# A layer's first projection from the raw stream, scaled per token where its result is read

## The reference

```python
# one layer; x is (256, 1024), norm_g[l] has 1024 weights
h = rmsnorm(x, norm_g)          # x * g / sqrt(mean(x*x) + 1e-6), the mean over a token's features
p = h @ w_in                    # (1024, 11168); its parts are, by column:
# conv branch | lora: 256 of q, 128 of kv, 32 of rope key | dilated q, k, v | gates
q_a  = rmsnorm(p_q,  q_a_norm_g)    # over 256
kv_a = rmsnorm(p_kv, kv_a_norm_g)   # over 128
... three branches (convolution, latent attention, dilated attention), their sum gated
x = x + merged @ w_o
```

## Time and profile before

| | |
|---|---|
| median of 3 runs | 1988.99 us (1988.62 to 1989.37) |
| the profiled execution | 1993.92 us, its span 1992.0 us |
| PE busy | 1888.7 us, 95% |
| DVE / ACT / POOL busy | 749.3 / 581.2 / 522.7 us |
| layers (PE's last sum of x) | to 817.0 us |

### The profile page before, as it was taken

One profiled execution on the slowest core, in us unless ns is written; L12 is line 12 of the kernel. 1 busy time (PEld: TensorE's weight loads), 2 busy tenths in 40 slices (PEclk: granted clock), 3 DMA queues, 4 the chain that ended last, 5 costly groups with the idle time before them and its releaser, 6 DMA issues.

```text
span 1992.0 us, 26961 instructions
## 1 busy us (share of the span) xinstructions
PE 1888.7 (95%) x10968; PEld 1193.8 (60%) x10968; DVE 749.3 (38%) x1417; ACT 581.2 (29%) x1051; POOL 522.7 (26%) x220
## 2 busy tenths in 40 slices
PE   7999999989999999989899999999999999999997
PEld 6779889977799899744474444343334443333443
DVE  4785563447854644544534212121112121211212
ACT  4554445445544455322412111011011110110111
POOL 5766556767674557200000000000000000000000
PEclk9999999999999999999989999999999999999999
DMA  8555333555553234621548999999999999999995
GB/s 304 191 174 207 128 107 118 205 182 201 181 194 134 97 127 170 221 85 43 206 157 367 429 427 430 428 428 429 428 429 427 428 428 428 429 428 429 428 429 234
DMA packets 111413, 563.43 MB, mean 283 GB/s; under 512 B 4768, under 2 KB 24352, under 8 KB 86464
## 3 DMA queue, kind: packets, MB, share of 16 engines
q1 hardware_dynamic: 111328, 562.21, 70.5%
HBM read 561.15 MB, written 1.05 MB: 282 GB/s over the span
## 4 chain that ended last, share of the span: by engine, by line
PE 61%; DMA 28%; DVE 7%; ACT 2%; issue 1%; SPq 0%; DVEq 0%; ACTq 0%
DMA ring<-in_e_in_dram 28%; PE bank L1708 15%; PE score L927 11%; PE bank L1698 10%; PE bank L749 4%; PE mixed L965 4%; PE bank L1675 3%; PE bank L850 2%; PE mixed L1792 1%; PE flip L1775 1%; DVE ring L2280 1%; PE bank L988 1%; PE score L1761 1%; PE score L948 1%; PE flip L1733 1%
## 5 line engine op out<-in xcount | busy, mean ns | idle before, releaser
L2087 POOL TENSOR_TENSOR w_lo<-ring,w_hi 128x1024 fp32r<-128x1024 f32 (+1 forms) x216 | 522.5, 2431 | 285.2 <-ACT w_hi L1986 284.6
L927 PE MATMUL score<-ring,space 128*64 128x512 f32 x2016 | 452.7, 594 | 38.4 <-DMA ring<-in_e_in_dram 37.2
L927 PEld LDWEIGHTS score<-ring,space 128*64 128x64 f32 x2016 | 141.6, 137 | 338.4 <-issue 248.6
L1986 ACT ACTIVATE w_hi<-ring 128x1024 fp32r<-128x1024 f32 (+1 forms) x216 | 226.8, 1051 | 219.3 <-PE bank L1708 120.5
L1708 PE MATMUL bank<-h_hi,w_hi 128*128 128x256 f32 x896 | 261.9, 292 | 0.0
L1708 PE MATMUL bank<-h_lo,w_hi 128*128 128x256 f32 x896 | 254.2, 284 | 0.0
L1708 PE MATMUL bank<-h_hi,w_lo 128*128 128x256 f32 x896 | 254.0, 283 | 0.0
L965 PE MATMUL mixed<-ring,space 128*64 128x512 f32 x1024 | 226.8, 595 | 0.3 <-ACT space L1183 0.3
L1179 ACT ACTIVATE space<-space 128x512 f32<-128x512 f32 x32 | 20.2, 632 | 695.7 <-DVE space L1482 695.7
L1482 DVE TENSOR_SCALAR space<-score 128x512 f32<-128x512 f32 x32 | 22.2, 693 | 411.1 <-PE score L927 411.1
L1708 PEld LDWEIGHTS bank<-h_hi,w_hi 128*128 128x128 f32 x896 | 172.6, 193 | 4.5 <-issue 4.4
(11 more groups left out here) (341 smaller groups left out, 2351.0 us busy)
## 6 DMA issues: line engine op xcount, KB each, us to landing
ring<-in_e_in_dram SPq DMA_DIRECT2D x126, 2048.0 KB, 25.1
ring<-in_e_out_dram SPq DMA_DIRECT2D x64, 2048.0 KB, 22.1
ring<-in_w_in_dram SPq DMA_DIRECT2D x42, 2048.0 KB, 7.8
ring<-in_w_ada_dram SPq DMA_DIRECT2D x16, 1024.0 KB, 5.3
ring<-in_w_o_dram SPq DMA_DIRECT2D x6, 2048.0 KB, 8.0
ring<-in_w_qkv_dram SPq DMA_DIRECT2D x4, 2048.0 KB, 10.0
ring<-in_w_ada_dram SPq DMA_DIRECT2D x4, 2048.0 KB, 7.9
ring<-in_w_out_a_dram SPq DMA_DIRECT2D x2, 2048.0 KB, 7.9
```

The lines of the kernel that those rows point to most:

```text
L927: ins = pe.matmul(score[HALF * blk:HALF * blk + HALF, which * W:(which + 1) * W], xs[:, 2 * j + r, HALF * hh:HALF * hh + HALF], wk[:, blk ...
L1986: act.activation(split_part(w_hi, k), raw_part(k), ACT.Copy).then_inc(hi_done, 1)
L2087: pool.tensor_tensor(split_part(w_lo, k), raw_part(k), split_part(w_hi, k), ALU.subtract).then_inc(lo_done, 1)
```

## The change

Lora reads a second pair of buffers, `raw_hi` and `raw_lo`: x times the norm's weights, without the token's scale, split. ACT makes the high half of a piece (two operations), DVE the low half (two). In layer 0 pieces 0 to 2 are made before the root; in layer 1 pieces 0 and 1 stand behind the second squares of x, together with the splits of quarters 0 and 1. The normed stream is made as before, for the units behind lora; in ACT's queue the splits of quarters 3, 4, 5, 6 now stand before its pieces 0, 1, 2, 3. The token's scale as a column, `token_rs`, comes from a product of `rsx` with the identity and a sum, behind the stream's last subtraction; the squares and the reads of lora's result take it in.

```diff
+        raw_hi, raw_lo = latent_r[:, 0:DC, :], latent_r[:, DC:2 * DC, :]
+        token_rs = stat[:, 1, 0:TT]
...
-                if kind in ("lora", "out"):
-                    pe.wait_ge(hready, l * 8 + (0 if kind == "lora" else 4) + q + 1)
+                if kind == "lora":
+                    pe.wait_ge(raw_ready, l * 4 + q + 1)
+                elif kind == "out" or QUARTER[u] == 4:
+                    pe.wait_ge(hready, l * 8 + (4 if kind == "out" else 0) + q + 1)
+                x_hi, x_lo = (raw_hi, raw_lo) if kind == "lora" else (h_hi, h_lo)
...
-                            for x_, w_ in ((h_hi, w_hi), (h_hi, w_lo), (h_lo, w_hi)):
+                            for x_, w_ in ((x_hi, w_hi), (x_hi, w_lo), (x_lo, w_hi)):
                                 ins = pe.matmul(b[:, 0:n], x_[:, c, t], w_[:, k % PARTS, i, 0:n],
-                                                start=c == 0 and x_ is h_hi and w_ is w_hi,
-                                                stop=c == DC - 1 and x_ is h_lo)
+                                                start=c == 0 and x_ is x_hi and w_ is w_hi,
+                                                stop=c == DC - 1 and x_ is x_lo)
...
+            def squares_of_both(l, u, width, scales=(1.0, 1.0)):
                 act.wait_ge(squares_used, l * NG + MEAN_OF[u] + 1)
                 act.wait_ge(unit_done, done(l, u))
-                act.activation(square2[:, 0, 0:width], bank_of(u)[:, 0:width], ACT.Square)
+                act.activation(square2[:, 0, 0:width], bank_of(u)[:, 0:width], ACT.Square, scale=scales[0])
                 act.wait_ge(unit_done, done(l, u + 1))
-                act.activation(square2[:, 1, 0:width], bank_of(u + 1)[:, 0:width], ACT.Square).then_inc(squares, 1)
+                act.activation(square2[:, 1, 0:width], bank_of(u + 1)[:, 0:width], ACT.Square,
+                               scale=scales[1]).then_inc(squares, 1)
...
-                        squares_of_both(l, u, 384 if kind == "lora" else W)
+                        if kind == "lora":
+                            act.wait_ge(token_ready, l + 1)
+                            squares_of_both(l, u, 384, [token_rs[:, t:t + 1] for t in range(TT)])
+                        else:
+                            squares_of_both(l, u, W)
...
+            def raw_high(l, i):
+
+                layer_now[0] = l
+                for c in (2 * i, 2 * i + 1):
+                    ins = act.activation(raw_hi[:, c, :], x[:, c, :], ACT.Copy, scale=l_("norm_g", c, 1))
+                ins.then_inc(raw_rounded, 1)
+
             for i in range(4):
                 squares_of_x(0, i)
             act.wait_ge(ones_ready, 1)
             act.activation(stat[:, 0, 15:16], ones[:, 0:1], ACT.Sqrt)
             act.wait_ge(par_ready, 1)
+            for i in range(3):
+                raw_high(0, i)
+            split_to(0, 1)
             for l in range(LAYERS):
                 layer_now[0] = l
-                split[0] = 0
                 act.wait_ge(score_free, l * NS + 2)
                 act.activation(rsx, varx, ACT.Sqrt).then_inc(rsx_ready, 1)
+                raw_high(l, 3)
+                split_to(l, PARTS)
                 for n in range(4):
-                    split_to(l, min(n + 1, PARTS))
+                    split_to(l, PARTS + n + 1)
                     stream_high(l, n, normed_x)
                 evacuate(l, 0)
                 for u in range(HEAD, PREP):
@@ -2073,6 +2099,14 @@
                         act.wait_ge(bpar_loaded, 32)
                         act.activation(ctx_squares, ctx_x, ACT.Square).then_inc(bsquared, 1)
                     squares_of_x(l + 1, i)
+                    if l + 1 < LAYERS and i == 1:
+                        raw_high(l + 1, 0)
+                        raw_high(l + 1, 1)
+                        split[0] = 0
+                        split_to(l + 1, 2)
+                if l + 1 < LAYERS:
+                    split_to(l + 1, PARTS)
+                    raw_high(l + 1, 2)
...
+            def raw_low(l, i):
+                now, layer_now[0] = layer_now[0], l
+                dve.wait_ge(raw_rounded, l * 4 + i + 1)
+                for c in (2 * i, 2 * i + 1):
+                    ins = dve.scalar_tensor_tensor(out=raw_lo[:, c, :], in0=x[:, c, :], scalar=l_("norm_g", c, 1),
+                                                   in1=raw_hi[:, c, :], op0=ALU.mult, op1=ALU.subtract)
+                ins.then_inc(raw_ready, 1)
+                layer_now[0] = now
+
+            def token_scales(l):
+
+                own = qn[0][:, 0:T].rearrange("p (t n) -> p t n", t=TT)
+                link(dve.tensor_tensor(own, rsx.rearrange("p (t n) -> p t n", t=TT),
+                                       c_("ident").unsqueeze(1).broadcast_to([P, TT, P]), ALU.mult))
+                dve.tensor_reduce(token_rs, own, AX.X, ALU.add).then_inc(token_ready, 1)
...
-                    link(dve.tensor_copy(kpe[:, t, :], b[:, 384:416]))
-                    link(dve.tensor_scalar(q[:, 0:256], b[:, 0:256], rs[:, r:r + 1], None, ALU.mult))
-                    dve.tensor_scalar(q[:, 256:384], b[:, 256:384], rs[:, r + 1:r + 2], None,
+                    own = token_rs[:, t:t + 1]
+                    link(dve.tensor_scalar(kpe[:, t, :], b[:, 384:416], own, None, ALU.mult))
+                    link(dve.tensor_scalar(q[:, 0:256], b[:, 0:256], rs[:, r:r + 1], own, ALU.mult, ALU.mult))
+                    dve.tensor_scalar(q[:, 256:384], b[:, 256:384], rs[:, r + 1:r + 2], own, ALU.mult,
                                       ALU.mult).then_inc(free_of(u), 1)
...
+            for i in range(2):
+                raw_low(0, i)
             for l in range(LAYERS):
                 base[0] = l * PER["layer"] + start
                 steps[0] = 0
                 layer_now[0] = l
                 dve.wait_ge(scored, l * NS + 1)
                 dve.tensor_scalar(varx, score[:, 0:T], 1.0 / D, EPS, ALU.mult, ALU.add).then_inc(score_free, 1)
+                raw_low(l, 2)
                 dve.wait_ge(rsx_ready, l + 1)
                 link(dve.reciprocal(rsx, rsx))
+                raw_low(l, 3)
                 for n in range(4):
                     for c in (2 * n, 2 * n + 1):
                         ins = dve.scalar_tensor_tensor(out=normed_x[:, c, :], in0=x[:, c, :], scalar=l_("norm_g", c, 1),
@@ -2359,6 +2414,7 @@
                 stream_low(l, 3, normed_x)
                 if l == 0:
                     dve.wait_ge(loaded, 16)
+                token_scales(l)
                 for u in range(PREP):
                     evacuate(l, u)
                 for j in range(NJ + 1):
@@ -2386,6 +2442,9 @@
                 dve.wait_ge(free_of(FILL - 1), freed(l, FILL - 1))
                 dve.wait_ge(free_of(FILL - 2), freed(l, FILL - 2))
                 for u in range(FILL, NU):
+                    if l + 1 < LAYERS and u == NU - 2:
+                        raw_low(l + 1, 0)
+                        raw_low(l + 1, 1)
```

More of the change, by code:

```diff
@@ L215 @@
 CP, NCP = places(CONSTS)
-CHAINED = dict(layer=111, pair=2, job=2)
+CHAINED = dict(layer=112, pair=2, job=2)
 def slope(g, h):
@@ L452, in build @@
         hready = sem("hready")
+        raw_rounded = sem("raw_rounded")
+        raw_ready = sem("raw_ready")
+        token_ready = sem("token_ready")
         unit_done = sem("unit_done")
@@ L1866, in squares_of @@
                 act.activation(square[:, 0:width], src, ACT.Square).then_inc(squares, 1)
-            def squares_of_both(l, u, width):
+            def squares_of_both(l, u, width, scales=(1.0, 1.0)):
                 act.wait_ge(squares_used, l * NG + MEAN_OF[u] + 1)
                 act.wait_ge(unit_done, done(l, u))
-                act.activation(square2[:, 0, 0:width], bank_of(u)[:, 0:width], ACT.Square)
+                act.activation(square2[:, 0, 0:width], bank_of(u)[:, 0:width], ACT.Square, scale=scales[0])
                 act.wait_ge(unit_done, done(l, u + 1))
-                act.activation(square2[:, 1, 0:width], bank_of(u + 1)[:, 0:width], ACT.Square).then_inc(squares, 1)
+                act.activation(square2[:, 1, 0:width], bank_of(u + 1)[:, 0:width], ACT.Square,
+                               scale=scales[1]).then_inc(squares, 1)
             def root(l, u):
```

## The result

Slower by 0.57%: the ratio of the changed kernel's runs to those of before is 1.0057 with an interval of 1.0045 to 1.0068, from 8 runs each (medians 2002.17 and 1989.39 us). The profiled executions took 2001.8 and 1993.92 us, 7.9 apart (spans 2000.0 and 1992.0). A second series, on another chip, gave 1.0044 (1.003 to 1.0057). By the two ratios the loss is 9 to 11 us, by their intervals 6 to 14; the forecast was 7.5. The eight runs of the kernel before lie in two groups, five at 1988.6 to 1989.4 us and three at 1994.7 to 1995.3, and its profiled execution lies near the upper one, so the profiled pair shows less of a loss than the medians (12.8).

What follows compares the result with a forecast made beforehand. TensorE, busy for 95% of the span, was taken to bound the kernel. Waits of 2.6 (layer 1) and 3.1 (layer 0) plus clock 2.0 gave 7.7 us on 1988.99, so 1996.7, forecast as 1996.5; range 1986 to 2001.

Steps and rivals of the forecast that it cites:

- main step: In both layers, VectorE operations with two SBUF inputs wait for GpSimd's running split; one gets through between two splits.
- the lead of unit 1: Lora's earlier start without waiting for the normed stream: 16.95 instead of 18.5 in layer 0, 3.0 us ahead in layer 1.
- Q7: Quarter 7, the eighth of the layer, on TensorE; forecast 2.6 us late in layer 1, 2.4 to 3.8 in layer 0.
- Waits, 5.7 us in the sum: Delay at Q7 from VectorE's waits behind splits: 2.6 us in layer 1 and 3.1 in layer 0.
- the second of the two cases: Layer 0, clock back 3.4 us earlier than before: Q7 at 41.3, 2.4 late, instead of 42.7, 3.8 late.
- The lead in layer 1: Unit 1 (lora) of layer 1 starts at 417.8, 3.0 us ahead; its lead is 5.7 if nothing behind it waited.
- Clock: TensorE at half clock behind the new waits before the turn and Q7: 1.0 us a layer, 2.0 in all, none to 3.4.
- Q7's shift as the whole's: Each microsecond by which Q7 moves counts as one of the whole time.
- the stream isn't held up: Second rival: stream done at 429.2 in layer 1, Q7 4.8 us sooner there, 1.2 in layer 0; time 1983, chance 0.09.
- more than one operation fits between two splits: First rival: two of three VectorE waits per layer go, 2.0 us each, sum about 0; time 1986 to 1992, chance 0.19.
- the third rival: Half clock in full (3.4), or low halves later by one split each (2.4 a layer): 10 to 13 us, 2000 to 2002, chance 0.10.
- my forecast proper: The whole kernel's time at 1996.5 us, between 1992.5 and 1999.5, chance 0.62.

Runs made afterwards that it cites:

- e1_psum: The changed kernel with the reciprocal written to PSUM and read there by the stream operations and the product with the identity; ratio 1.0004 (0.9995 to 1.0012).
- e2_before_psum: The kernel before the change with the reciprocal written to PSUM, nothing else; ratio 0.9970 (0.9958 to 0.9982).
- e11_after_split7: The changed kernel with split 7 ahead of the squares and the root of lora's result in ScalarE's queue, nothing else; ratio 1.0044.

## Why the prediction was right

**The place and the sign.** Its main step held: the lead of unit 1 is given back by waits of VectorE for GpSimd. Unit 1 was forecast for 17.0 and measured at 16.85; subtraction 3 was forecast to end at about 35 and ended at 33.7; Q7 at 41.3 to 42.7 and came at 40.84. In layer 1, where the changed kernel arrives 2.7 us late, the forecast moves to 420.5, 439.1 and 446.6; measured were 421.95, 439.08 and 446.23.

**Waits, 5.7 us in the sum, measured 4.3** (1.96 and 2.3). One operation of the stream waited behind each of splits 3, 4, 5 and 6, in both layers, as I had counted. In layer 1 the stream's end came as forecast. In layer 0 it came 1.6 us sooner (33.70, not 35.3), for two reasons. The clock was back at 18.30, not at 21.47 as in the kernel before, the second of the two cases between which the forecast took the middle (its Q7: 41.3); so split 3 came sooner, and subtraction 0 ended at 23.8, not 25.1. And I had GpSimd busy without a pause from split 4 to 6; it paused for 1.97 us ahead of split 6, while ScalarE too waited for VectorE, and four operations ran free in the pause.

**The lead in layer 1, forecast 3.0, measured 1.6.** Behind the sums' wait (2.4 us) the granted clock was 0.50 from 417.67 on, so sums and ada rows took longer. It made no difference further on: the low half of piece 2 waited 0.4 us, not the 1.6 of the forecast, and the reciprocal ended at 424.23 (forecast, moved by 2.7: 424.2).

**Clock, 2.0 in the sum, measured 4.6** (2.2 and 2.4), less 1.4 for a stretch elsewhere. This is the term that I had too small: 6.82 us at half clock in each layer, not 3.4, and Q7 with most of its 12 matmuls in it. The run with TensorE kept busy puts it at 4 to 7 us. With waits and clock off in opposite directions, the sum of 7.7 met the profiled 7.9 better than its parts did; that is luck.

**Q7's shift as the whole's.** Held in this pair of profiles: 7.4 behind Q7 of layer 1, 8.0 at the last matmuls. In other pairs it was off by 4 to 5 us. Against the same profile of the kernel before, the repeated change stands 9.4 later behind Q7 of layer 1 and 4.6 later at its last matmuls; e1_psum 2.1 later and then 1.5 sooner; e2_before_psum 3.3 sooner and then 7.0. In between, stretches at half clock fall differently from one execution to the next.

**The rivals.** That the stream isn't held up is refuted by the rows of 2 us and more. That more than one operation fits between two splits came true only in the pause of 1.97 us; the waits stayed. Of the third rival, longer waits by a split were not seen, but its half clock in full was, and more (4.6 us against its 3.4), and its time, 2000 to 2002, is the one that was met: the median of the runs, 2002.17, lies 1.2 us above the range's end, the ratio times the median before at 2000.3 within it. Both are above the 1999.5 at which my forecast proper ended; only the second series, at 1.0044, would come to 1997.7 in it. So the range held in part because it took in half of that rival, to which I had given 0.10. Half-clock stretches that differ between executions of one kernel go with the spread of the runs (granted clock 0.988 in the run of 1997.33, 0.983 in that of 2006.22).

## What to carry to other kernels

Work that is brought forward to fill an engine's wait must be counted at the resource that two others share: here nine more operations with two SBUF inputs in each layer came beside GpSimd's splits. Look which inputs a VectorE operation takes from SBUF while GpSimd runs: moving one operand of eight operations a layer to PSUM made the kernel before 0.30% faster, and brought the change back to level with it (1.0004). And a wait of TensorE of 3 us can cost 2.2 to 2.4 us more behind it, at half clock; it doesn't always, so read the granted clock behind each wait. A profile is of one execution: here its total is good to a few microseconds, and a step's own shift is told better at the place of the change.

## What the runs showed of the hardware

A VectorE operation that comes while a GpSimd subtraction of 2.4 us runs took 2.39 us even with 64 elements a partition, and two with the second input in PSUM took 0.86 together beside such a subtraction (at 22.46 and 25.49 in e1_psum). Reading lora's result with two per-partition scalars instead of one costs 0.06 us more: 0.54 against 0.48 for 256 elements, 0.41 against 0.35 for 128. A half-clock stretch followed waits of 3.7 us in all (2.86 and 0.82) in layer 0. None followed a single wait of 3.07 us in layer 0 of e11_after_split7, nor the waits for splits of up to 1.6 us when the stream stood ahead of the splits. One also came without a wait: in the kernel before the clock was at 0.50 for 3.4 us from 195.54, behind 32 matmuls of 128x2 (3.63 us from 190.35) and a few more small ones.
